# A decoder block on eight cores: when the first weight slot and the memory tiles are asked for, and where the last tile is transposed

## The reference, cut to what matters

```python
h = rms_norm(x, norm_mix)
proj = h @ w_in                    # (B, S, 8*1024)
b_a, c_a, u_a, u_p, q_x, g_a, g_p, g_x = split(proj)
y_a = (b_a * causal_depthwise_conv(c_a * u_a, conv_w)) @ w_conv_out
y_p = einsum(multiscale_causal_pool(u_p), w_pool) * pool_scale
y_x = memory_cross_attention(q_x, rms_norm(mem, norm_mem), w_kv) @ w_xattn_out
x = x + (sigmoid(g_a)*y_a + sigmoid(g_p)*y_p + sigmoid(g_x)*y_x) @ w_out
h = rms_norm(x, norm_ffn)
x = x + (silu(h @ w_gate) * (h @ w_up)) @ w_down
return rms_norm(x, norm_final)
```

## Time and profile before

| | us |
|---|---|
| median of 3 runs | 1140.46 (1140.18 to 1140.6) |
| the profiled execution, its own time | 1147.27 |
| its span, slowest core (core 3) | 1145.7 |
| spans of the other seven cores | 1136.1 to 1139.3 |
| PE busy on core 3 | 1121.7 (98%) |
| DVE, ACT, POOL busy | 475.8, 305.6, 79.1 |

### The profile page before, as it was taken

The page is one execution under the profiler, slowest core; times in us unless marked ns, Lnnn a source line. Parts: engine busy times, 40 slices in busy tenths (PEclk is TensorE's granted clock), DMA queues, the critical chain, the costliest instruction groups (busy, mean ns, idle before and its releaser), DMA issues.

```text
span 1145.7 us, 14700 instructions; the slowest of 8 cores (1136.1 to 1145.7 us)
## 1 busy us (share of the span) xinstructions
PE 1121.7 (98%) x5574; PEld 542.3 (47%) x5574; DVE 475.8 (42%) x482; ACT 305.6 (27%) x490; POOL 79.1 (7%) x153
## 2 busy tenths in 40 slices
PE   7999999998999999999999999999999999999998
PEld 3666545453454444444444444444444444444444
DVE  5453554553656556553545622111334211111223
ACT  5434444224212323421212110112432111111111
POOL 1110100100100010001000101111000000000000
PEclk9999999998999999999999999999999999999999
DMA  9999881688498989335415543999967354200133
GB/s 244 172 203 162 132 206 47 114 147 107 83 191 195 258 150 173 61 106 111 76 39 107 95 142 103 219 175 173 173 154 193 102 126 77 37 1 1 37 112 109
DMA packets 78916, 146.34 MB, mean 128 GB/s; under 512 B 46571, under 2 KB 46571, under 8 KB 78592
## 3 DMA queue, kind: packets, MB, share of 16 engines
q0 software_dynamic: 21456, 77.64, 40.1%
q1 hardware_dynamic: 57392, 67.78, 21.7%
HBM read 185.27 MB, written 23.07 MB: 182 GB/s over the span
## 4 chain that ended last, share of the span: by engine, by line
PE 90%; DMA 4%; DVE 3%; ACT 1%; issue 1%; SPq 0%; DVEq 0%; ACTq 0%
PE ps L228 90%; DMA arena<-hb 3%; DMA arena<-x 1%; ACT tmp L419 1%; DVE tmp L390 0%; DVE hb L331 0%; DVE tmp L470 0%; DVE smx L416 0%; PE ps L343 0%; DVE tmp L383 0%; DVE arena L397 0%; ACT tmp L387 0%; ACT hA L352 0%; SPq L177 0%; DVE tmp L483 0%
## 5 line engine op out<-in xcount | busy, mean ns | idle before, releaser
L228 PE MATMUL ps<-hA,ring 128*128 128x512 bf16 (+3 forms) x2496 | 509.0, 364 | 9.1 <-DMA ring<-w_in 5.1
L228 PEld LDWEIGHTS ps<-hA,ring 128*128 128x128 bf16 x2496 | 243.7, 98 | 266.8 <-issue 14.2
L228 PE MATMUL ps<-arena,ring 128*128 128x512 bf16 (+1 forms) x1600 | 330.7, 366 | 0.8 <-ACT tmp L419 0.8
L228 PEld LDWEIGHTS ps<-arena,ring 128*128 128x128 bf16 x1600 | 156.5, 98 | 170.5 <-issue 1.1
L228 PE MATMUL ps<-arena 128*128 128x512 bf16 (+1 forms) x854 | 181.3, 374 | 0.0
L629 DVE TENSOR_TENSOR arena<-ps,tmp 128x1024 bf16<-128x1024 f32 x44 | 53.9, 1225 | 227.9 <-PE ps L228 223.9
L228 PEld LDWEIGHTS ps<-arena 128*128 128x128 bf16 x854 | 83.5, 98 | 96.3
L625 ACT ACTIVATE tmp<-ps 128x1024 f32<-128x1024 f32 x44 | 45.1, 1025 | 253.5 <-PE ps L228 253.5
L470 DVE TENSOR_TENSOR tmp<-tmp 128x1024 f32<-128x1024 f32 (+6 forms) x40 | 49.2, 1230 | 41.1 <-ACT tmp L460 38.6
L228 PE MATMUL ps<-ring,arena 128*128 128x512 bf16 x256 | 57.9, 379 | 0.2 <-issue 0.2
L218 POOL DMA_DIRECT2D ring<-w_in x48 | 25.6, 541 | 442.3 <-PE ps L228 333.4
(11 more groups left out here) (98 smaller groups left out, 585.3 us busy)
## 6 DMA issues: line engine op xcount, KB each, us to landing
ring<-w_in POOLq DMA_DIRECT2D x48, 512.0 KB, 12.9
ring<-w_gate_up POOLq DMA_DIRECT2D x44, 512.0 KB, 12.2
arena<-x SPq DMA_DIRECT2D x32, 512.0 KB, 7.2
tmp<-x_scr SPq DMA_DIRECT2D x24, 512.0 KB, 4.8
x_scr<-arena SPq DMA_DIRECT2D x16, 512.0 KB, 3.3
out<-tmp SPq DMA_DIRECT2D x15, 512.0 KB, 3.1
arena<-w_down POOLq DMA_DIRECT2D x11, 512.0 KB, 24.6
ring<-w_kv POOLq DMA_DIRECT2D x8, 512.0 KB, 18.6
```

Of the source, the lines that this page charges most:

```text
L228: ins = e.matmul(o, l, r, start=s0, stop=s1)
```

## The change

Three edits. Slot 0 is asked for when x tile 0 has landed (`kXs(0)`), no longer at once. The gain of the memory norm is asked for when x tile 6 has landed (`kXs(6)`); the two memory tiles stand behind it in SP's queue. And tile 7 (index 8) is transposed ahead of `uc[1].block(1)`, no longer behind it, and its bank is copied by DVE, no longer by ACT.

```diff
-    cs[0] = conv_slots(0, ((), kXs(5), kXs(7)))
+    cs[0] = conv_slots(0, (kXs(0), kXs(5), kXs(7)))
...
-    load_gain(1, 1)
+    spd(gBs[1][:, :], gains_d[1], kXs(6), [("gB", 1)])
     for mt in range(2):
         spd(xb(2 + mt), mem_d[mt * P:(mt + 1) * P, :], [], kX(2 + mt))
...
     a2(8)
     ax(7)
     ae(7, False)
+    ax(8)
+    ae(8, True)
     uc[1].block(1)
-    ax(8)
-    ae(8, False)
     for u in uc:
         u.block(2)
```

## The result

| | before | after |
|---|---|---|
| median, same chip | 1140.53 us | 1153.2 us (1152.58 and 1153.89) |
| profiled execution, its own time | 1147.27 us | 1152.58 us |
| its slowest core | core 3, 1145.7 us | core 2, 1151.0 us |
| the other seven cores | 1136.1 to 1139.3 us | 1139.0 to 1145.7 us |

The changed kernel is slower: 1.0111 times the time before, 95% interval 1.0094 to 1.0128. I had forecast 1138.0 us, in a range up to 1140.4. Executions in which one die's cores ran at a lower granted clock than the other's (two of the changed kernel, up to 1180.73) are left out of every ratio and median, and where cores 0 to 3 had it through a whole session, cores 4 to 7 alone are compared.

A forecast was written before the change was run, and what follows sets the result against it. PE was taken to bound the kernel, the end following block(2)'s start: 3.7 us earlier less a 1.25 us wait for slot 2 gives -2.45, so 1140.46 - 2.45 = 1138.0 us, range 1136.4 to 1140.4.

The forecast's parts named there:

- What bounds the kernel: PE is 90% of the chain of waits; the end moves one for one with block(2)'s start, if nothing behind waits anew.
- Tile 7's part: Before block(2): tile 7 transposed ahead of the second block(1) and copied by DVE starts block(2) 0.9 us earlier.
- Slot 0 later: At the start: tile 0 lands at 5 to 5.5, slot 0 at 15.7 to 18.7, block(0) starts at about 17.7.
- Block(2): On core 5, PE's first-half block(2) starts at 29.15 instead of 32.89, 3.7 us earlier.
- Slot 2 as the new wait: After block(2) on core 5, PE wants weight slot 2 at 34.55, has it at 35.8, and waits 1.25 us.
- Gain and memory tiles later: SP's requests deferred to 21 to 23 us: landing 1 us later, between nothing and 3; cost nothing, range 0 to 2.
- the memory tiles bind: Rival, chance 0.06: memory tiles 3 us later hold DVE's product and PE's bank by 1.5 us, time 1139.6.
- The accident of core 3: Weight slot asked for at 257.27, its matmuls start at 275.71 after 5.13 us of PE idling; left out of the sum.
- The rule against it: SWDGE descriptor starvation while DVE copies: slot 0 up to 1.28 us later, at 20 at worst, block(2) by about that.

## Why the prediction was wrong, point by point

- **What bounds the kernel.** Right that PE alone counts, and that the end follows the start one for one: behind the block of 40 the cores of both kernels take 1089.3 to 1089.9 us, but for the three named. But I set the point too early, at block(2), and wrote "if nothing behind it waits anew".
- **Tile 7's part.** 0.9 us foreseen, 1.05 measured alone, on the median core.
- **Slot 0 later.** Half right. x tile 2 came earlier, its square on core 5 at 11.55. But tile 0 landed at 7.9 there, not at 5 to 5.5; slot 0, asked for at 8.42, took 11.4 us to 19.8, and my landing of 15.7 to 18.7 was counted from a request at 5.5. PE waited 3.04 us, and block(0) took 4.58 us at the low clock again. The whole edit gave 0.25 us alone.
- **Block(2).** It starts at 31.66 on core 5 (the row at 30.36 has 1.30 of block(1) in it), 1.2 us earlier, not 3.7. So the forecast would have come out too low even without the step below: with the memory request back, the median core gains 1.2 us, not 2.45, and the best execution is 1139.66, not 1138.0.
- **Slot 2 as the new wait.** Not seen on core 5. The largest wait for a slot between block(0) and 45 us on any core of the changed kernel is under 1 us.
- **The step that failed** is "Gain and memory tiles later": "I estimate a landing 1 us later, between nothing and 3 us. I take nothing for it". It was 9.2 us later on core 5 (2.5 to 11.0 on the others), with 4.3 us of wait and 2.1 of slow clock behind it, and 6.0 us of the median core when the edit stood alone. The error is in the words "the queue of x before it is only just empty then". I took an empty queue ahead of a request for no loss. It is the loss: the transfers that used to keep the engines busy in that gap are pushed to where POOL's slots compete, and holding four of those slots back took most of PE's wait away. The rival "the memory tiles bind" was the right mechanism, with 0.06, but priced at 1.5 us from 3 us of lateness, and without the low clock. The rows I had could have told: in the same stretch slot 2 alone took 12.3 us, and the second memory tile stands behind two transfers of that size. One such landing after the request at 21.6 was its floor, 34, and with two more in front of it 40 was likely; its square, root and scaling are 3.3 us, and PE wants them at 40.
- **The accident of core 3.** I left it out of the sum as a weight slot that came late once. It is a mechanism of the kernel: in 14 of 23 executions of the last session the kernel before has a core over 1145, by its size this event, and the profiled execution of the changed kernel is 5.3 us longer for it (core 2 at 1151.0 over core 7 at 1145.7). That the three runs shown of before had none was luck, and the forecast is counted from them: 1140.46 is what this kernel takes when no core is struck.
- **The rule against it** (POOL starved of descriptors by DVE): no sign of it. Slot 0's request at 8.42, with DVE busy from 8.32, took 0.53 us.

## What to carry to other kernels

A request that is deferred "until it is needed" leaves the list of what the DMA engines have to do. Before deferring, look at what the queue holds at that moment: if it is about to be empty when the request comes, the bytes are paid for later, beside whatever else is queued then; here it was enough to put the wait on a transfer that is still two or three from the end. Work ahead of a wait that is set by a DMA is worth nothing until that wait is gone, so look for the next such wait before adding up gains. And a core that is late once in a profile is worth following to its first cause, past the releaser that the row names.

## What the runs showed that I had not expected

- A transposing DMA of SP has two durations. In the 16 profiles of eight cores, 128 cases of `b_trans(3)`, it landed 3.1 to 7.6 us after its request in 97, and 10.9 to 21.0 us after in 31. All 31 were asked for no earlier than 1.4 us before POOL's request of the slot `w_p_t`, the second of a burst of five slots; all 97 at least 1.0 us before it. That it goes with the burst is read off the traces; why it takes so long is open, and no run here has the transpose beside a single slot.
- What puts a core on the wrong side of that burst is not shown, nor why most of the variants had it in nearly every execution of the first two sessions, and the kernel before in 24 of 55.
- SP's gain, 512 KB, needs 5.7 to 13.1 us when it is asked for behind tile 6 with only tile 7 still on its way, and on core 5 of the changed kernel, asked for at 21.24, moves its first packets in number only from 26 us on, while the engines moved 115 GB/s.
